# A two-layer block with an MLP on one Trainium2 core: the up and down products issued over 256 tokens instead of 512

## What is computed

```python
D_MODEL, SEQ, D_FF = 1024, 512, 4096

m = rms_norm_2(h, g_mlp_pre[i]) @ w_up[i]
m = jnp.square(jax.nn.relu(m)) @ w_down[i]
h = h + rms_norm_2(m, g_mlp_post[i])

gate = jax.nn.sigmoid(h @ w_ple_gate[i])
e = rms_norm_2(p[i] @ w_ple_proj[i], g_ple[i])
h = h + gate * e
```

## Time and profile before

| | |
|---|---|
| runs of the kernel before | 1564.22, 1565.81, 1569.62 us |
| median | 1565.81 us |
| span of the profiled execution | 1562.4 us (its own time is not given; the median lies 3.4 us above the span) |
| busy: PE, PE weight loads | 1531.7, 1222.0 us |
| busy: DVE, ACT, POOL | 893.4, 751.1, 258.1 us |
| mean traffic | 81 GB/s |

### The profile page before, as it was taken

The page is one execution under the profiler, slowest core; times in us unless marked ns, Lnnn a source line. Parts: engine busy times, 40 slices in busy tenths (PEclk is TensorE's granted clock), DMA queues, the critical chain, the costliest instruction groups (busy, mean ns, idle before and its releaser), DMA issues.

```text
span 1562.4 us, 20671 instructions
## 1 busy us (share of the span) xinstructions
PE 1531.7 (98%) x7650; PEld 1222.0 (78%) x7650; DVE 893.4 (57%) x1681; ACT 751.1 (48%) x1310; POOL 258.1 (17%) x453
## 2 busy tenths in 40 slices
PE   9989999999999999999998999999999999999998
PEld 7878888888878777777776887666678888888877
DVE  5767677776656456666666435554375243443476
ACT  4454455544553346666667314656555241332343
POOL 1033323443313003343343000000000000000000
PEclk9999999999999999999999999999999999999999
DMA  5311111211114332222222231112222223233221
GB/s 202 109 54 54 55 54 55 67 55 55 47 48 153 99 106 73 84 82 68 81 76 68 81 108 63 54 68 68 67 85 91 94 95 108 84 105 95 94 95 54
DMA packets 40163, 127.22 MB, mean 81 GB/s; under 512 B 4576, under 2 KB 9104, under 8 KB 40064
## 3 DMA queue, kind: packets, MB, share of 16 engines
q1 hardware_dynamic: 38112, 121.65, 24.1%
q0 software_dynamic: 1040, 3.27, 0.6%
q10 hardware_dynamic: 912, 0.99, 0.2%
HBM read 122.69 MB, written 2.15 MB: 80 GB/s over the span
## 4 chain that ended last, share of the span: by engine, by line
PE 90%; DVE 5%; ACT 3%; POOL 1%; issue 1%; DMA 0%; SPq 0%; POOLq 0%; ACTq 0%; DVEq 0%
PE ps L833 87%; PE ps L1196 2%; PE ps L976 1%; DVE wl L1945 1%; ACT L L1751 1%; POOL L L2761 1%; DVE h L2595 1%; DVE mo L2589 1%; POOL uc L2731 0%; POOL masks L2729 0%; DVE L L2452 0%; DVE up L2080 0%; DMA wraw<-in_wa 0%; DVE xm L2582 0%; ACT wh L1340 0%
## 5 line engine op out<-in xcount | busy, mean ns | idle before, releaser
L833 PE MATMUL ps<-xr,wh 128*128 128x512 f32 x2752 | 880.1, 401 | 3.5 <-DVE xr L2388 1.2
L833 PEld LDWEIGHTS ps<-xr,wh 128*128 128x128 f32 x2752 | 505.7, 188 | 129.6 <-issue 30.5
L833 PE MATMUL ps<-xr,wl 128*128 128x512 f32 x1376 | 538.4, 391 | 0.0
L1945 DVE TENSOR_TENSOR wl<-wraw,wh 128x1024 fp32r<-128x1024 f32 x214 | 264.5, 1243 | 130.9 <-ACT wh L1340 128.8
L833 PEld LDWEIGHTS ps<-xr,wl 128*128 128x128 f32 x1376 | 258.6, 188 | 56.1
L1340 ACT ACTIVATE wh<-wraw 128x1024 fp32r<-128x1024 f32 x214 | 222.2, 1049 | 85.8 <-PE ps L833 83.8
L833 PE MATMUL ps<-xm,wh 128*128 128x512 f32 x640 | 198.8, 392 | 5.1 <-DVE xm L2582 2.7
L833 PEld LDWEIGHTS ps<-xm,wh 128*128 128x128 f32 x640 | 119.5, 188 | 33.5 <-DVE xm L2582 4.0
L2761 POOL TENSOR_SCALAR L<-L,m 128x256 f32<-128x256 f32 (+1 forms) x128 | 99.2, 794 | 272.2 <-DVE m L2467 272.2
L833 PE MATMUL ps<-xm,wl 128*128 128x512 f32 x320 | 124.7, 390 | 0.0
L1983 DVE SCALAR_TENSOR_TENSOR qkv<-cin,gains,qkv 128x512 f32<-128x512 f32 x96 | 77.3, 807 | 10.6 <-ACT qkv L1370 9.7
(11 more groups left out here) (265 smaller groups left out, 1749.7 us busy)
## 6 DMA issues: line engine op xcount, KB each, us to landing
wraw<-in_wa SPq DMA_DIRECT2D x48, 512.0 KB, 3.7
wraw<-in_wb SPq DMA_DIRECT2D x32, 512.0 KB, 4.0
wraw<-in_wu SPq DMA_DIRECT2D x32, 512.0 KB, 3.6
wraw<-in_wd SPq DMA_DIRECT2D x32, 512.0 KB, 3.7
wraw<-in_wao SPq DMA_DIRECT2D x16, 512.0 KB, 3.7
wraw<-in_wbo SPq DMA_DIRECT2D x16, 512.0 KB, 3.9
wraw<-in_wc SPq DMA_DIRECT2D x16, 512.0 KB, 3.7
bias<-rel_rows SPq DMA_DIRECT2D x16, 256.0 KB, 3.8
```

What stands on the lines that cost most here:

```text
L833: return e.matmul(out, w, x, start=start, stop=stop, skip_group_check=True)
L1945: e.tensor_tensor(m.wl[:, i % N_SPLIT, :], m.raw[:, i % N_RAW, :], m.wh[:, i % N_SPLIT, :].bitcast(F), ALU.subtract).then_inc(s.wlo, 1)
```

## The change

`mm3_halves` issues the three matmuls of a piece for the tokens 0 to 255, then the same three for the tokens 256 to 511, with the same weights, into the left and the right half of the bank. Only the very first of a bank has the start flag (the right half's first matmul has not). The last matmul is the one returned, so it carries the signal of use. It is taken for `up` and `down`; all other products stay with `mm3`.

```diff
@@ -837,6 +837,14 @@
         mm(bank, wa, xb, False, False)
         return mm(bank, wb, xa, False, last)
 
+    def mm3_halves(bank, wa, wb, xa, xb, first, last):
+        for at in (0, 256):
+            t = slice(at, at + 256)
+            mm(bank[:, t], wa, xa[:, t], first and at == 0, False)
+            mm(bank[:, t], wa, xb[:, t], False, False)
+            ins = mm(bank[:, t], wb, xa[:, t], False, last)
+        return ins
+
     def cleared(b):
         for sem, v in clear[b]:
             e.wait_ge(sem, v)
@@ -911,7 +919,8 @@
                     e.wait_ge(s.wlo, i + 1)
                 if n == 0:
                     await_piece(name, k, a)
-                ins = mm3(out, wh, wl, *X[k], first, last)
+                three = mm3_halves if name in ("up", "down") else mm3
+                ins = three(out, wh, wl, *X[k], first, last)
                 if kk == 7:
                     ins.then_inc(s.wused, 1)
             elif what == CLOSE:
```

## The result

The changed kernel takes 1589.1 us (median of 4 runs, 1587.46 to 1589.53), the kernel before 1567.5 us (4 runs, 1564.22 to 1569.62). The ratio is 1.0136 with a 95% interval of 1.0116 to 1.0156, so the change costs 21.6 us between the medians. The forecast was 1585.8 us, +20.0, in a range of 1562 to 1608.

The account below looks back on a forecast made before the run. The prediction took TensorE (PE), busy without gaps in the MLP, to bound the kernel. 1500 passes at 13.3 ns add 20.0 us, all else nothing, so 1565.8 + 20.0 = 1585.8 us, range 1562 to 1608.

Parts of the forecast that it names:

- PE is the bound and the added time arrives in full: MLP: PE busy 325.00 of 325.00 us, so whatever is added to the distance between matmul starts reaches the end in full.
- Columns and loads cost nothing: up and down: same number of columns; 1536 more weight loads covered by the matmul beside them, floor 111.5 ns under 120.
- 13.3 ns belong to the matmul: Settled MLP stream: 226.7 ns less 213.3 of columns is paid per matmul, so a half costs 120.0 ns, a pair 240.0.
- a handover between matmuls: Hint from matmuls after a wait, 230 ns each: what varies with the queue's history is a handover, not a streaming rate.
- The argument against it: Plain float32 shows hardly any handover, 0.86 us for 0.853 of columns, so the full rate of streaming may be what costs.
- The load is excluded as the cause: The 16-column wab loads last 93 to 98 ns instead of 188, yet their matmuls take 233 ns each, no less.
- 1500 passes count, +20.0 us: up and down: 1536 passes less 36 standing before PE's last wait for x, each 13.3 ns slower, +20.0 us.
- One (columns): Same 1500 passes: the 13.3 ns go with the columns streamed, so not slower, 1565.8 us or down to 1560.3; chance 0.26.
- Two (unsettled): MLP: PE stays in the state after a wait, 126.7 ns a half, +40 us, 1606 us; chance 0.09.
- Three (issue): MLP: instruction issue is the limit at 153 ns a pair, +119 us, 1685 us; chance 0.04.
- Four (load no longer beside): MLP: weight loads stop lying beside the matmul, 118 ns a half more, +354 us, 1920 us; chance 0.03.
- The check by 0.72 us for two triples and the mean record of 283 ns: MLP timeline: two triples of halves span 0.72 us instead of 0.68 for one of 512; mean record falls from 389 ns.

Follow-up runs that it names:

- quarters: Matmuls of up and down cut into four of 128 columns, against the kernel before with 512: 1943.7 us beside 1567.3; repeated, 1943.25 us.
- the uneven cuts: Matmuls of up and down cut into 320 and 192 columns, against the kernel before with 512: 1614.95 us beside 1569.9.
- the contiguous operand: Kernel before with up on bfloat16 views, two of three matmuls taking their moving operand from a contiguous view of a constant tile: 1564.2 us beside 1564.1.
- narrow_load: Kernel before at 512 columns; in up and down two of three matmuls load and use 64 of 128 weight columns: 1569.95 us beside 1564.1.
- bf16_high: Kernel before with up's 512-column matmuls on a bfloat16 view of the same tiles, every second element: 1565.85 us, ratio 0.9988.

## Why the prediction was right

- *PE is the bound and the added time arrives in full.* Right: one PE piece of 364.62 us, full clock, one wait of 0.4 us.
- *Columns and loads cost nothing.* Right. Loads still start with the matmul before them; their floor is 111.7 ns, shown by the quarters, and 120 lies above it. (The prediction has 111.5 from the earlier trace rows, where 0.89 us over eight are 111.3; it makes no difference to the forecast.)
- *13.3 ns belong to the matmul.* Right in size, 120.0 ns; the uneven cuts (257.8 against 258.2 ns) exclude the share of columns. As for the reason, the prediction had only a hint, that matmuls behind a wait stand further apart, and took it for a handover between matmuls. No run bears that reading out as the cause of the settled 13.3 ns, so the choice between the two, held at 0.58, was right with some luck. What the runs show is narrower: 12 to 13 ns with four-byte steps at the full clock, under 2 ns on the contiguous operand. The argument against it, that the full rate of streaming might be the cause, was half right: it depends on how the operand is read, but once a matmul, not once a column.
- *The load is excluded as the cause,* from the 16-column loads of wab: borne out by narrow_load, where shorter loads bring no gain, and by bf16_high, with 225 ns beside load records of 96.
- *1500 passes count, +20.0 us.* The chain says 19.9. The medians say 21.6, or 20.2 with the clock taken off. The profiled spans say 24.5, of which 4.7 lie ahead of the MLP, mostly in the lower clock at 430 to 450 us. The measured 1589.1 lies 3.3 us above the forecast time: 1.7 of it is the base, a median of 1567.5 instead of the 1565.8 of three runs, and 1.6 the difference of the medians. The prediction expected the same times ahead of 1148 us and a clock of 1.00 in the slices; this was wrong for this execution, and has nothing to do with the change.
- *The rivals.* One (columns) fell with the uneven cuts. Two (unsettled) fell: the halves stand 120.0 ns apart, by the start times in the trace over all of 1180 to 1500 us. Three (issue) fell: 120 ns a pair for 365 us without gaps. Four (load no longer beside) fell.
- The check by 0.72 us for two triples and the mean record of 283 ns came out as written.

## What to carry to other kernels

Where TensorE is busy without gaps, read the distance of starts in the timeline and take off the columns at the granted clock: what remains is paid again by every further matmul, so keep the moving operand at 512 columns, above all where its elements are four bytes apart. Above the floor of a weight load of 128 float32r columns (here 111.7 ns, which is 13.3 ns and 236 columns) a cut costs only this remainder; below it every cut costs a load. The price measured in the settled stream of the MLP was an upper bound in the other stages of this kernel, where the products come in short runs. And before a difference of a few us is read from times, set the runs side by side at the same mean granted clock: here this turned +5.2 us into +9.4.

## What the runs showed of the hardware beyond that

At the lower clock the remainder is gone. The kernel after at 439 us:

```profile
439.27 0.63 PE L833 MATMUL ps<-xr,wl 128*128 128x512 f32 x1
439.70 1.84 PE L833 MATMUL ps<-Tm,Mm 128*128 128x64 f32 x8
...
442.30 0.63 PE L833 MATMUL ps<-xr,wl 128*128 128x512 f32 x1
442.73 1.80 PE L833 MATMUL ps<-U,Pm 128*128 128x64 f32 x8
```

The next matmul starts 0.43 us later in both places, which is 512 columns at 1.2 GHz (426.7 ns) with nothing over; with 13.3 ns more it would be 0.44. So the 13.3 ns are a matter of the full clock, as of the four-byte step. At the lower clock the load's distance is longer too: in quarters nine 128-column matmuls take 1.92 us there (1200.06 to 1201.98 us), 213 ns each instead of 111.7.

Matmuls of few columns near waits can cost the clock: 85 to 89 us at half of it in both runs of the quarters, none with 256, 320 and 192, or 512 columns at the same place.
